# Held weight loads, first up parts on VectorE, and unread TensorE products ahead of an expert loop

## The reference, cut to what matters

```python
h2 = rms_norm(x, norm2_g) * (1 + sc2) + sh2
g_logits = t @ rg_w + rg_b                  # 4 groups, the best one is taken
e_logits = t @ re_w + re_b                  # 4 experts in a group, the best two are taken
...
for e in range(N_EXPERTS):
    he = jax.nn.silu(t @ w_gate[e]) * (t @ w_up[e])
    out = out + dense_w[:, e:e + 1] * (he @ w_down[e])
x = x + g2 * out
```

## Time and profile before

| | |
|---|---|
| median of 3 runs | 820.2 us (819.59 to 821.53) |
| the profiled execution, its own time | 821.15 us |
| its span, first to last instruction | 819.4 us |
| TensorE busy | 717.1 us (88%) |
| VectorE busy | 512.9 us (63%) |
| ScalarE busy | 396.2 us (48%) |
| GpSimd busy | 241.9 us (30%) |
| mean granted clock of TensorE | 0.943 of the high level |
| bytes moved | 196.36 MB, mean 240 GB/s |

### The profile page before, as it was taken

One profiled execution on the slowest core, in us unless ns is written; L12 is line 12 of the kernel. 1 busy time (PEld: TensorE's weight loads), 2 busy tenths in 40 slices (PEclk: granted clock), 3 DMA queues, 4 the chain that ended last, 5 costly groups with the idle time before them and its releaser, 6 DMA issues.

```text
span 819.4 us, 9897 instructions
## 1 busy us (share of the span) xinstructions
PE 717.1 (88%) x3634; PEld 567.3 (69%) x3634; DVE 512.9 (63%) x664; ACT 396.2 (48%) x484; POOL 241.9 (30%) x145
## 2 busy tenths in 40 slices
PE   2889999989999999998999239999999999999820
PEld 1566777767778777787787227888888888888610
DVE  0435643370456544774534948899999989999727
ACT  4322322312446365422224427777777777777423
POOL 0413342323253232356746450122111112200030
PEclk9999999989999999999999559999999999999865
DMA  8949656457432332283213949999999999994253
GB/s 326 318 128 364 181 165 204 153 187 209 114 93 71 84 78 52 78 321 108 81 48 131 431 182 342 421 412 418 408 401 415 409 410 413 410 411 171 107 193 139
DMA packets 78105, 196.36 MB, mean 240 GB/s; under 512 B 13430, under 2 KB 46366, under 8 KB 71416
## 3 DMA queue, kind: packets, MB, share of 16 engines
q1 hardware_dynamic: 66432, 160.51, 53.7%
q0 software_dynamic: 5696, 21.88, 7.3%
q10 hardware_dynamic: 5944, 13.52, 5.0%
HBM read 179.07 MB, written 16.83 MB: 239 GB/s over the span
## 4 chain that ended last, share of the span: by engine, by line
PE 65%; issue 10%; DVE 8%; DMA 7%; ACT 5%; POOL 2%; SPq 1%; POOLq 0%; DVEq 0%; ACTq 0%
PE psum L766 54%; PE psum L842 3%; DMA slots<-ada_w 2%; ACT xbuf L1357 2%; DMA h_rows<-rot_pT 2%; PE psum L1116 2%; PE psum L974 1%; DMA front_ring<-w_in 1%; ACT xbuf L1364 1%; PE psum L852 1%; DVE xbuf L1751 1%; DVE stat L1756 1%; POOL merged_low L2270 1%; POOL low_ring L2229 1%; ACT high_ring L1265 1%
## 5 line engine op out<-in xcount | busy, mean ns | idle before, releaser
L2229 POOL TENSOR_TENSOR low_ring<-front_ring,high_ring 128x1024 fp32r<-128x1024 f32 x52 | 128.2, 2466 | 253.0 <-ACT high_ring L1265 253.0
L1265 ACT ACTIVATE high_ring<-front_ring 128x1024 fp32r<-128x1024 f32 x52 | 54.9, 1056 | 196.5 <-PE psum L766 132.6
L1460 ACT ACTIVATE chunk_high<-front_ring 128x2048 fp32r<-128x2048 f32 x48 | 91.8, 1919 | 43.3 <-DVE inout L2126 37.9
L766 PE MATMUL psum<-chunk_high,xsT_low 128*128 128x512 f32 x264 | 107.0, 405 | 5.9 <-DVE inout L2126 2.7
L766 PE MATMUL psum<-h_low,high_ring 128*128 128x512 f32 x296 | 111.2, 394 | 0.0
L766 PE MATMUL psum<-chunk_high,xsT_high 128*128 128x512 f32 x264 | 104.9, 397 | 0.0
L766 PE MATMUL psum<-h_high,low_ring 128*128 128x512 f32 x232 | 94.5, 407 | 3.2 <-DVE h_low L1654 2.7
L766 PE MATMUL psum<-h_high,high_ring 128*128 128x512 f32 x232 | 90.5, 390 | 0.0
L1460 ACT ACTIVATE chunk_high<-slots 128x2048 fp32r<-128x2048 f32 x32 | 60.4, 1910 | 20.0 <-PE psum L766 10.6
L2320 POOL COPY ids_now<-ids 128x1 uint32 x12 | 16.5, 1378 | 163.2 <-PE psum L1116 163.2
L766 PEld LDWEIGHTS psum<-h_low,high_ring 128*128 128x128 f32 x296 | 56.3, 190 | 11.0
(11 more groups left out here) (317 smaller groups left out, 1497.7 us busy)
## 6 DMA issues: line engine op xcount, KB each, us to landing
front_ring<-w_down SPq DMA_DIRECT2D x16, 2048.0 KB, 10.0
front_ring<-w_in SPq DMA_DIRECT2D x34, 512.0 KB, 5.8
xbuf<-ada_w SPq DMA_DIRECT2D x32, 512.0 KB, 4.6
slot<-w_gate SPq DMA_DIRECT2D x8, 2048.0 KB
slots<-w_up SPq DMA_DIRECT2D x8, 2048.0 KB, 10.0
slots<-w_gate SPq DMA_DIRECT2D x8, 2048.0 KB, 10.1
front_ring<-w_up SPq DMA_DIRECT2D x8, 2048.0 KB, 9.6
y_rows<-inout ACTq DMA_DIRECT2D x16, 512.0 KB, 9.4
```

The costliest lines, as they stand in the source:

```text
L766: mm = pe.matmul(out, lhs(a, k), rhs(b, k), start=(start and k == 0 and a == 1), stop=(stop and k == count - 1 and (a, b) == (0, 0)))
L1265: act.activation(dst, src.rearrange("p (k n) -> p k n", k=KD), ACT.Copy).then_inc(high_ready, 1)
L1460: act.activation(chunk_high[place], raw_chunk(q, which, j), ACT.Copy).then_inc(chunk_split, 1)
L2229: pool.tensor_tensor(low, src, high.bitcast(F32), ALU.subtract).then_inc(low_ready, 1)
```

## The change

SP keeps two of the five loads ahead of the loop where they were and puts the other three behind a wait for the gathered rows of tile 0. GpSimd's two up subtractions go to VectorE, between `low_part` of tile 0's gate and `count_tiles`. TensorE gets products of two constants into a PSUM bank that nobody reads: eight before the wait for `onehots_ready`, two before `ids`, five before the first `turn_x`.

```diff
-            load_in(1, 1, 0)
-            load_down(0, 0)
-            sp.wait_ge(h2_pool, TT - 1)
-            sp.wait_ge(h2_dve, 1)
-            load_in(1, 1, 1)
+            sp.wait_ge(xs_landed[0], 16)
+            load_in(1, 1, 0)
+            load_in(1, 1, 1)
+            load_down(0, 0)
...
+            def keep_going(count):
+                for _ in range(count):
+                    pe.matmul(psum[:, 6, :], ident, early[:, 0:COLS], start=True, stop=True)
...
+            keep_going(8)
             pe.wait_ge(onehots_ready, 1)
...
+            keep_going(2)
             name = "ids"
             wait_bank(pe, name)
...
+            keep_going(5)
             turn_x(0, 0, 1)
...
-            pe.wait_ge(pool_low, 1)
+            pe.wait_ge(first_up_low, 1)
             expand_chunk(0, 0, 1, 0, 2)
-            pe.wait_ge(pool_low, 2)
+            pe.wait_ge(first_up_low, 2)
             expand_chunk(0, 0, 1, 1, 3)
...
+            def first_up_part(j, place):
+                dve.tensor_tensor(low_chunk(0, 1, j), raw_chunk(0, 1, j), chunk_high[place].bitcast(F32),
+                                  ALU.subtract).then_inc(first_up_low, 1)
...
             low_part(0, 0, 1, 1)
+            for j in range(2):
+                dve.wait_ge(chunk_split, 3 + j)
+                first_up_part(j, 2 + j)
             count_tiles()
...
-            for j in range(2):
-                pool.wait_ge(chunk_split, 3 + j)
-                low_chunk_part(0, 1, j, 2 + j)
```

More of the change, by code:

```diff
@@ L516, in hybrid_layer @@
         dve_low = sem("dve_low")
-        pool_low = sem("pool_low")
+        first_up_low = sem("first_up_low")
         second_low = sem("second_low")
@@ L2301, in gather @@
                                         bass.IndirectOffsetOnAxis(ap=idx, axis=0)).then_inc(xs_landed[q], 16)
-            def low_chunk_part(q, which, j, place):
-                pool.tensor_tensor(low_chunk(q, which, j), raw_chunk(q, which, j), chunk_high[place].bitcast(F32),
-                                   ALU.subtract).then_inc(pool_low, 1)
             pool.wait_ge(h2_stored, 16 * TT)
```

## The result

| | before | after |
|---|---|---|
| median | 820.87 us (8 runs: seven from 816.68 to 821.69, one of 1254.36) | 813.28 us (8 runs, 809.88 to 816.54) |
| profiled execution, its own time | 821.15 us | 813.78 us |
| its span | 819.4 us | 812.0 us |
| mean granted clock of TensorE | 0.943 | 0.957 |

The ratio is 0.991, with a 95% interval of 0.9892 to 0.9928: faster by some 7.4 us, with 813.4 forecast for the median. The run of 1254.36 us is left out of the ratio; without it the median before is 820.2.

The account below looks back on a forecast made before the run. TensorE's split products bound it, except between routing and the first expert product, where a store waits behind queued loads. First product 6.75 us earlier, off 821.15, gives 814.4; less 0.95 to the median, 813.4; range 810.7 to 816.4.

Parts of the forecast that it names:

- The hold: SP's loads ahead of the loop: fourth store lands after 2.6 to 4.4 us, gather issued at 469.8, landed at 475.3.
- the sum: Terms up to the first expert product: `ids` cast 469.56 + 0.23, gather from 469.8, first product at 480.4, 6.75 us earlier.
- What is late next: Ahead of the first product: VectorE, done at 479.6, is later than transposes and copies, at 478.6, by a microsecond.
- The unread products: TensorE's waits before the first product: taken as 0, between 1.65 and 1.1 us gained and 0.8 and 1.5 lost.
- lay beside other work: GpSimd's two up parts, 4.54 us each: TensorE did not wait for them; without the move, first product about 479.4.
- rival 2: Gather starves behind four VectorE subtractions, lands at 483.1, first product 487.1: 820; chance 0.07 together with rival 5.
- Behind the first product: Tile 1's gate, issued 475.4, lands some 7 us later, 482.5; 3.7 us more of queue are absorbed in the loop.
- a sign that I had listed as wrong: In the expert loop: waits of ScalarE for tile 1's or 2's loads would show the forecast wrong.
- 1 (transfers bound the loop): Expert loop: 46 loads from 475.4 against 43 from 494.3 leave 4.3 us of gain, 815.9; chance 0.07.
- 4 (a late release is lost at the end): Held 6.3 MB hang on the gather: landed at 483.1, loads end 3.5 us later, 823.7; chance 0.06.
- 3: Unread products at the low level delay rank, `ids` and transposes: first product at 486.2, 819.3; chance 0.03.
- 5: Fourth store stays slow for its own reason, gather stays at 478.7, time as rival 2's; chance 0.07 together with rival 2.

Follow-up runs that it names:

- e6: The changed kernel with the three held loads released once the four stores have landed (`h2_stored`), not at tile 0's gathered rows: 819.42 us, ratio 0.9984.
- e5: The changed kernel without the unread products, so hold and move only: 813.29 us, ratio 0.991 to the kernel before.
- e8: The changed kernel with 11, 3 and 7 unread products instead of 8, 2 and 5, and three more behind the transposes: 809.85 us, ratio 0.9883.
- e1: The kernel before with SP's hold of the three loads alone: 817.73 us, ratio 0.9977.
- e4: The changed kernel with the two up parts still on GpSimd, so hold and unread products only: 817.34 us, ratio 0.9953 to the kernel before.
- e7: The changed kernel with the three held loads released at the second tile's gathered rows (`xs_landed[1]`): 811.48 us, ratio 0.9896.
- e9: The changed kernel with the second up part put behind `split_x` on VectorE's list: 811.0 us, ratio 0.9898.
- e11: The changed kernel with the up parts still on GpSimd and `count_tiles` put behind `split_x`: 809.0 us, ratio 0.9874.
- e2: The kernel before with the unread products alone (8, 2 and 5): 820.46 us, ratio 1.0003.
- e3: The kernel before with the move of the two up parts to VectorE alone: 819.74 us, ratio 0.9996.

## Why the prediction was right, and where it was not

**The hold** went as worked out. The store landed after 2.9 (2.6 to 4.4 forecast), the gather left at 470.03 with an issue of 2.11 (2.16), and its rows landed at 475.4 (475.3). That last agreement is luck: the cast began 0.73 earlier than in the sum, and the gather started 1.2 behind the start of the cast, in every trace with the hold, where the sum had 0.24. e6 shows that the point of release, not the hold as such, decides: the loads must wait for the rows, not for the store.

**What is late next** was VectorE, as forecast, and by the forecast chain: four subtractions in a row, `count_tiles`, `split_x`. The first product stood at 479.56, 0.84 ahead of 480.4; from the fixed point it is 1.26 ahead (17.35, not 18.61). Of that, 1.15 is the cast (6.62 behind the fixed point, not 7.77), because the `ids` products took 1.90 at the high level instead of 3.65. The other side, ready at 477.7, beat 478.6 since transposes and copies took 1.16 and 1.09. VectorE's lead of a microsecond hangs on that level: in e5, with the cast where the sum has it and transposes of 1.96, ScalarE was done at 480.71 and `count_tiles` at 480.69, a tie, as the gather's late start was not in the sum.

**The unread products** I took at 0, between 1.65 and 1.1 gained and 0.8 and 1.5 lost. e5 against the changed kernel gives 0.991 for both. In single traces they gave 1.23 at the first product and took 0.33 in the first 48, so 0.9 where the sum has 0. That the median came within 0.2 of the forecast is luck too: the runs spread over 6.7 us, and terms of a microsecond cancelled. The level fell in both gaps, as expected. That it could be held, and is worth 1.8 us, is e8's.

**The step that was wrong** is a sentence that the sum did not need: that what the move removes "lay beside other work", and that without the move the first product would stand at "about 479.4". e1 and e5 differ by the move alone, their casts are alike (7.77 and 7.76 behind the fixed point), and without the move the first product came 4.7 us later (23.26 against 18.58). e4 against the changed kernel says the same: 6.5 later (23.83 against 17.35), of which 1.7 is its late cast, and the rest the scan's 9.35 less its usual 0.19 and less the 4.40 of the two subtractions that VectorE was spared. GpSimd's subtractions lie beside TensorE's work, but not beside VectorE's: the scan of `count_tiles` is held for as long as they run. The move is not a cost that the hold pays for; it is half of the change. I had weighed the rule that tells of it, in the Trainium skill, page "SBUF — State Buffer", section "SBUF: two separate sides" (a VectorE operation with two inputs in SBUF and a GpSimd operation that reads SBUF shut each other out of the shared port pair), against the gather alone, and not against GpSimd's own subtractions beside VectorE's list. The page tells the starved transfer of VectorE operations in a two-port mode, which such subtractions do not have by it, so it spoke less for rival 2 than I took it to. The scans of e1 and e4 agree with the rule, and go further: they were held for two instructions, not one. The trace of before had the sign of it, off the path in a cast of 16 numbers beside GpSimd's parts of the earlier trace rows, and on the path in the ranking (VectorE in time order, then GpSimd's third block of `h2`):

```profile
487.56 2.49 DVE L2055 CAST tile_table<-mvb 1x16 int32<-1x16 f32 x1
...
489.98 0.16 DVE L2056 CAST tile_table<-mvb 1x16 int32<-1x16 f32 x1
...
458.51 2.95 DVE L1981 TENSOR_TENSOR mvb<-mvb 128x64 f32<-128x64 f32 x2
...
462.00 0.33 DVE L1988 TENSOR_TENSOR mvb<-mvb 128x64 f32<-128x64 f32 x2
...
458.88 2.35 POOL L2290 TENSOR_TENSOR rot_pT<-front_ring,mqk 128x1024 f32<-128x1024 f32 x1
```

The same cast takes 2.49 and 0.16, the longer one until GpSimd is done; two operations of one shape take 2.95 beside GpSimd and 0.33 without it. Lines 1967 and 1974 took 2.52 and 1.84 beside GpSimd's blocks in the same way. By these rows the ranking is held for some 6 us (an estimate), in both kernels and ahead of the fixed point; what freeing it is worth was not tried.

**Behind the first product**, tile 1's gate took 11.1 us to land, not 7 (the terms named for it give 6.3): issued at 475.38, there at 486.5 instead of 482.5, and ScalarE waited 8.84 for it, a sign that I had listed as wrong:

```profile
486.53 1.92 ACT L1467 ACTIVATE chunk_high<-slots 128x2048 fp32r<-128x2048 f32 x1 [8.84 <-DMA slots<-w_gate]
```

It cost nothing: e7, where that wait is 10.20, is no slower. The reason stays open. The engines moved only 248 GB/s from 475 to 480, and from 474 to 478 mostly gathered rows (0.77 MB, against 0.20 of the loads); the three loads landed after 11.1, 16.1 and 20.6, the later two some 5 apart, so it is the first that is late. The loop itself took 11.05 for tile 2's products and no transfer held ScalarE there, so 3.7 us of queue were absorbed, as forecast.

**The rivals.** 1 (transfers bound the loop) and 4 (a late release is lost at the end) fall with e7. 2 (the gather starves) falls with 2.11 and 5.3; but its port is real and held VectorE instead of GpSimd. 3 was seen in two traces, e9 and e4, at less than a third of its price. 5 falls with the store's 2.9.

## What to carry to other kernels

A small transfer on the path is paid for by what is queued ahead of it: hold large loads until the last small one has landed, not until the one before it. When a step moves forward in time, look at what it now runs beside: an operation that was harmless on another engine can hold a tiny one on the path, and the row to look for is a small operation with a large time. Then first ask whether the held operation has to be there: moving it (e11, one line) did no less than moving the work.

## What the runs showed of the hardware

- A VectorE scan of 128x16 with both inputs in SBUF was held for two GpSimd subtractions of 128x2048 in a row, 9.35 us instead of 0.19 (e1, e4): it did not get in between the two. A cast with its one input in SBUF was held too (2.49 instead of 0.16, before). VectorE operations with an operand in PSUM were not held at all (1.29 and 0.17 in e11).
- The GpSimd issue of a gather took 2.10 to 2.11 beside VectorE's two-input subtractions and 1.02 without (e2): a microsecond, no more.
- Behind 6 MB of loads, 512 KB took 11.8 us (e6), and behind some 8 MB 14.0; with them held, 2.9 and 5.3.
- Eight transposes between products did not keep TensorE's level (0.79 from 476 to 477 in the changed kernel, 0.50 after); with three unread products behind them, and two more ahead, it stayed at 1.00 (e8). It also stayed in e9, where the unread products ran right up to the transposes and 1.97 us without work lay behind these. 48 products took 11.25 at the high level throughout, and 12.6 to 13.9 where it had to come back (e2, e3).
